# Gate-row indices, the row order of the modulation table, and the order of Pool's gathers and scatters in a mixture-of-experts stage

## The chip, the cores and the metric

The kernel runs on one core of a Trainium2 chip. The metric is the device time of one execution in microseconds (us). Before the change the median of three runs is 1618.47 us (1617.96 to 1618.78).

## The reference, cut to what matters

One decoder layer runs on 1024 prompt tokens and on 32 sample tokens (8 sequences of 4). A vector `c`, one for the prompt and one for each sample sequence, gives nine rows of modulation through `silu(c) @ w_ada + b_ada`: shift, scale and gate for the token mixers, and shift `sh2`, scale `sc2` and gate `g2` for the experts. After the mixers:

```python
h2 = rms_norm(x, norm2_g) * (1 + sc2) + sh2
y  = hier_moe(h2)                 # best group of 4, best 2 of its 8 experts, SwiGLU experts
x  = x + g2 * y                   # g2: one row for the prompt, one for each sample sequence
y_out = rms_norm(x, final_norm_g)
```

There are 32 experts with weights `w1`, `w3` (1024 x 512) and `w2` (512 x 1024) in float32, 6 MB for each expert. The 1056 tokens make 2112 assignments, 66 for an expert on average. With the inputs of this reference the lists are 24 to 172 tokens long.

## The kernel before, in words

The mixers run first, in two halves. The last stage, about 960 to 1616 us in the profile, is the expert stage: `moe_sync` (SyncE's queue, loads of weights), `moe_gpsimd` (Pool: indirect gathers and scatters), `moe_tensor`, `moe_scalar` and `moe_vector`. Each engine has its own list of instructions, in the order in which the code calls them, and waits on semaphores.

The stage goes through NB = 33 blocks of 128 slots. Blocks 0 to 31 are one for each expert, with its tokens in the first partitions, in the order of the tokens, and padding behind them (a padded slot holds token number 2047). Block 32 takes the rest of a list longer than 128. For a block `b`:

- Pool gathers the 128 token rows from `h2_rows` into `xg` (line 796, `gather`). Padded slots are out of bounds and are skipped.
- TensorE transposes them (line 904), ScalarE and VectorE split the result into a high part `xTh` and a low part `xTl`.
- Four chunks of `w1`/`w3` and two of `w2`, 1 MB each, come over SyncE's queue into a ring of 13 buffers `wr` (line 664). ScalarE rounds each to `whr` (`high`, line 1103), VectorE forms the rest `wl` (`low`, the helper at line 1288). TensorE multiplies three times for each product (lines 913 to 915 for the up part, 930 to 932 for the down part). A load waits until TensorE has freed its buffer.
- ScalarE multiplies the row of `g2` of each slot, held in `g2p`, by the slot's routing weight, into `gfac` (`factors`, line 1091). In block b's turn it does so for block b-1, ahead of two to four `high`. VectorE multiplies the product by `gfac` into `ysb` (`result`).
- Pool adds `ysb` to the residual rows `x_rows` in DRAM (line 800, `scatter`, an accumulating scatter).

`g2p` is one buffer. It is filled once with the prompt's row of g2 (line 849), and from then on it is patched: before each block an indirect gather (`gate_gather`, line 815) reads, by the index column `g2i[:, b]`, only the partitions whose row must change. Index 27 and above is out of bounds (`bounds_check=26`) and leaves the partition as it is. The source `gate_rows` is `mod_dram`, nine rows of three sections of 1024 (sh2, sc2, g2), seen as 27 rows: row 3n + 2 is the g2 of source n.

`gate_index` (line 1385) works out the indices. For 32 blocks at once it runs at the end of VectorE's block 0, just ahead of the `gate()` product of block 0 that TensorE waits for; for block 32 it runs once more in block 28. A slot with a sample token gets that sample's row; any other slot gets row 2 (the prompt) where the block before had a sample token in that partition, and else 30, which is skipped. So padding behaves as a prompt token does.

Pool's order is written out by hand. After the first three token gathers, for each block b: the token gather of b+3; for b = 0 the gate gather of block 0; the gate gather of b+1, once ScalarE has done factors(b); two table writes in blocks 3 to 11 (line 791); the scatter of b, once VectorE has done result(b). Behind the scatter of block 30 there stand a small weight gather (line 811), two gathers of residual rows (line 830) that wait for that scatter to land, and the gate gather of block 32. SyncE's loads of the residual tiles `yt` wait for the same scatter. The final norm and the stores follow.

Of the kernel before, what the change touches and what calls it, by code (L numbers as in the profile page):

```python
# [15 lines left out]
F32 = mybir.dt.float32  # L16
F32R = mybir.dt.float32r
BF16 = mybir.dt.bfloat16
I32 = mybir.dt.int32
U32 = mybir.dt.uint32  # L20
ALU = mybir.AluOpType
# [59 lines left out]
def build(nc, x_prompt, x_sample, c_prompt, c_sample, state_conv_a, state_conv_c, norm1_g, norm2_g,  # L81
# [5 lines left out]
    with ctx:  # L87
# [235 lines left out]
        eps, o = at("eps", [P, 1], F32, o)  # L323
# [47 lines left out]
        fss = sb("fss", [P, F_N])  # L371
        fv = sb("fv", [P, F_N])
        fr = sb("fr", [P, F_N])
        fy = sb("fy", [P, F_N])
        ft = sb("ft", [P, F_N])
# [402 lines left out]
        def moe_gpsimd(pool):  # L778
# [70 lines left out]
            pool.dma_start(g2p[:], mod_dram[0:1, 2 * D:3 * D].to_broadcast([P, D])).then_inc(g2_in, 16)  # L849
            for b in range(NB):  # L850
                if b + 3 < NB:
                    gather(b + 3)
                if b == 0:
                    pool.wait_ge(*gate_ok)
                    pool.wait_ge(g2_in, 16)
                    gate_gather(0, g2_in)
                if b + 1 < NB:
                    pool.wait_ge(m_w, b + 1)
                    gate_gather(b + 1, g2_in)
                if b == 3:  # L860
                    pool.wait_ge(dst_ok, 1)
                    pool.wait_ge(tab_out, 16)
                if 3 <= b < NT + 3:
                    fill_table(b - 3)
                if b < NB - 2:
                    scatter(b)
                if b == NT:
                    pool.wait_ge(wk_ok, 3)
                    pool.dma_start(wtab.rearrange("(p t) w -> p (t w)", p=P),
                                   wps[:].rearrange("p k t -> p (k t)")).then_inc(bd_in, 16)  # L870
                if b == NE - 2:
                    pool.wait_ge(bd_in, WT_IN + 16)
                    weight_gather(bd_in)
                if b == NB - 3:
                    base_gather(NB - 2)
                    base_gather(NB - 1)
# [409 lines left out]
        def moe_vector(dve):  # L1286
# [19 lines left out]
            dve.memset(wsl[:], 0.0)  # L1306
            pick_groups(dve, PT, NT)
# [77 lines left out]
            def gate_index(out, tok, before, now, n):  # L1385
                r, o = rf[:, 0:n], bf[:, 0:n]
                dve.tensor_scalar(r.bitcast(I32), tok, float(SEQ - TS), 0.0, ALU.subtract, ALU.max)
                dve.tensor_scalar(now, tok, float(SEQ), None, ALU.is_ge)
                dve.drain()
                dve.tensor_scalar(r.bitcast(I32), r.bitcast(I32), 2, None, ALU.logical_shift_right)  # L1390
                dve.scalar_tensor_tensor(now, tok, float(TOK), now, ALU.is_lt, ALU.mult)
                dve.drain()
                dve.tensor_scalar(r, r.bitcast(I32), 3.0, 2.0, ALU.mult, ALU.add)
                if before is None:
                    dve.memset(o, 2.0)
                else:
                    dve.tensor_scalar(o, before, 2.0 - 30.0, 30.0, ALU.mult, ALU.add)
                dve.drain()
                tt(r, r, o, ALU.subtract)
                dve.drain()  # L1400
                tt(r, r, now, ALU.mult)
                dve.drain()
                return tt(out, r, o, ALU.add)
# [66 lines left out]
            for b in range(NB):  # L1470
# [34 lines left out]
                if b == 0:  # L1505
                    table_rows_of()
                    dve.memset(gsf[:, 0:1], 0.0)
# [13 lines left out]
                if b == NB - 2:  # L1521
                    dve.memset(eps[:], EPS)
# [42 lines left out]
            with dve.If(n > 0):  # L1565
                scattered(dve, NB - 1)
                with dve.Fori(0, n) as i:
# [3 lines left out]
                    gate_index(g2i[:, NE:NB], xtok[:], None, gsf[:, NB:NB + 1], 1)  # L1571
# [86 lines left out]
        def _(pool):  # L1658
# [69 lines left out]
            def mod_store(i):  # L1728
# [3 lines left out]
                pool.dma_start(mod_dram[:, (j - 6) * 512:(j - 5) * 512], modr[:, i % 2, :]).then_inc(mod_out[i % 2], 16)  # L1732
# [60 lines left out]
            for g in range(2):  # L1793
# [26 lines left out]
                pool.dma_start(B2[:], mod_dram[0:1, 0:D].to_broadcast([P, D])).then_inc(ab_in, 16)  # L1820
                pool.dma_start(A2[:], mod_dram[0:1, D:2 * D].to_broadcast([P, D])).then_inc(ab_in, 16)
                if g:
                    pool.wait_ge(alo_ok, 2 * CW)
                    pool.wait_ge(st_out, 16 * (3 + 2 * NS))
                    for k in range(2):
                        for n in range(NS):
                            pool.dma_start(xs_s[n * TS:(n + 1) * TS, :] if k else xA[SMP + n * TS:SMP + (n + 1) * TS, PT, :],
                                           mod_dram[1 + n:2 + n, k * D:(k + 1) * D].to_broadcast([TS, D])
# [1453 lines left out]
```

## Time and profile before

| | us |
|---|---|
| median of 3 runs | 1618.47 |
| the profiled execution's own time | 1616.88 |
| its span | 1615.1 |
| TensorE busy | 1559.6 |
| VectorE busy | 1259.0 |
| ScalarE busy | 803.2 |
| Pool busy | 365.0 |

A page of the profile gives each engine's busy time, the span in 40 slices, and the chain of work that ended last. A timeline row is: start, duration, engine, line, operation, output<-input, count, and in brackets the idle time of the engine before it with the releaser. A row of the windows view gives the length of the stretch, then for TensorE, its weight loads, VectorE, ScalarE and Pool the busy time with the number of instructions, then the granted clock of TensorE as a share of full speed, the mean busy share of the 16 DMA engines, and GB/s. A DMA row ends with the median time from issue to landing, and a transfer has landed when the last of its parts has.

### The profile page before, as it was taken

Reading aid. Unit: us, or ns where it says so; the run is one execution under the profiler, and the core shown is the slowest. Engines: PE = TensorE matmul, PEld = TensorE weight load, DVE = VectorE, ACT = ScalarE, POOL = GpSimd, SP = SyncE. Lnnn points to the kernel's source line nnn. Section 1 sums busy time; section 2 is a strip of 40 time slices with the busy share of each in tenths; the row PEclk is TensorE's granted clock in tenths of the full one; section 3 lists DMA queues with packets and bytes.
Section 4 is the critical chain, followed back from the end, with each engine's and each line's share of the span. In section 5 each row is a group of like instructions: output and inputs, shape, how many; then the busy total and the mean of one; then the engine's idle time right before and its main releaser. Section 6 shows DMA issues by size and latency. Waiting matters only on the chain.

```text
span 1615.1 us, 23296 instructions
## 1 busy us (share of the span) xinstructions
PE 1559.6 (97%) x9097; PEld 1336.2 (83%) x9097; DVE 1259.0 (78%) x1703; ACT 803.2 (50%) x874; POOL 365.0 (23%) x273
## 2 busy tenths in 40 slices
PE   5999999999999999999999998999999999999993
PEld 3777788878889999999999977888888888888771
DVE  4668887755838898887555569999999999999985
ACT  4222232334333223313243356888788788777773
POOL 2310000000000000002000202466655544543231
PEclk9999999999999999999999998999999999999997
DMA  9965223424434332234222657999999999999965
GB/s 341 318 200 181 80 86 90 139 79 148 129 91 144 118 88 77 78 88 139 78 79 87 214 198 295 374 382 387 386 369 376 381 382 377 383 384 370 370 223 230
DMA packets 219025, 361.01 MB, mean 224 GB/s; under 512 B 20166, under 2 KB 168742, under 8 KB 193562
## 3 DMA queue, kind: packets, MB, share of 16 engines
q1 hardware_dynamic: 196476, 323.10, 55.8%
q0 software_dynamic: 21792, 34.25, 7.4%
q10 hardware_dynamic: 646, 2.15, 0.3%
q8 instruction: 73, 1.20, 0.3%
q14 instruction: 38, 0.31, 0.1%
HBM read 363.16 MB, written 32.34 MB: 245 GB/s over the span
## 4 chain that ended last, share of the span: by engine, by line
PE 85%; DMA 6%; DVE 5%; issue 1%; DVEq 1%; ACT 1%; POOL 0%; POOLq 0%; SPq 0%; ACTq 0%
PE z L2934 16%; PE z L2936 16%; PE z L2935 16%; PE z L913 6%; PE z L915 6%; PE z L914 6%; DMA wr<-in_w_dram 3%; PE z L930 3%; PE z L932 3%; PE z L931 3%; PE q L2825 2%; PE q L904 2%; PE q L2844 1%; DVE conv L2354 1%; DMA ada_h<-in_w_ada_dram 1%
## 5 line engine op out<-in xcount | busy, mean ns | idle before, releaser
L1288 DVE TENSOR_TENSOR wl<-wr,whr 128x2048 fp32r<-128x2048 f32 x196 | 442.2, 2284 | 0.1
L1103 ACT ACTIVATE whr<-wr 128x2048 fp32r<-128x2048 f32 x196 | 372.3, 1912 | 75.0 <-DMA wr<-in_w_dram 37.8
L2934 PE MATMUL z<-h_hi,w_hi 128*128 128x272 f32 (+1 forms) x1248 | 406.7, 326 | 2.3 <-DVE h_lo L2173 1.8
L2936 PE MATMUL z<-h_hi,w_lo 128*128 128x272 f32 (+1 forms) x1248 | 402.5, 322 | 0.0
L2935 PE MATMUL z<-h_lo,w_hi 128*128 128x272 f32 (+1 forms) x1248 | 401.3, 322 | 0.0
L2173 DVE TENSOR_TENSOR w_lo<-w_raw,w_hi 128x1024 fp32r<-128x1024 f32 (+1 forms) x168 | 179.4, 1068 | 127.4 <-ACT w_hi L1872 127.4
L2934 PEld LDWEIGHTS z<-h_hi,w_hi 128*128 128x128 f32 x1248 | 234.7, 188 | 28.3 <-issue 7.4
L2936 PEld LDWEIGHTS z<-h_hi,w_lo 128*128 128x128 f32 x1248 | 234.4, 188 | 16.6
L2935 PEld LDWEIGHTS z<-h_lo,w_hi 128*128 128x128 f32 x1248 | 234.8, 188 | 15.6 <-issue 0.2
L913 PE MATMUL z<-whr,xTh 128*128 128x512 f32 x528 | 209.9, 397 | 0.4 <-DVE xTl L1288 0.4
L915 PE MATMUL z<-wl,xTh 128*128 128x512 f32 x528 | 207.1, 392 | 0.0
L914 PE MATMUL z<-whr,xTl 128*128 128x512 f32 x528 | 206.5, 391 | 0.0
L2354 DVE SCALAR_TENSOR_TENSOR conv<-a_in,parT,conv 128x512 f32<-128x512 f32 x360 | 193.8, 582 | 14.5 <-issue 1.3
L1872 ACT ACTIVATE w_hi<-w_raw 128x1024 fp32r<-128x1024 f32 (+1 forms) x168 | 150.3, 929 | 48.1 <-DMA w_raw<-in_w_in_dram 48.0
L2050 ACT ACTIVATE sig<-z 128x512 f32<-128x512 f32 (+1 forms) x48 | 29.3, 611 | 264.9 <-PE z L2936 264.9
L815 POOL DMA_INDIRECT g2p<-mod_rows,g2i x33 | 82.8, 2509 | 250.6 <-ACT gfac L1091 232.9
L915 PEld LDWEIGHTS z<-wl,xTh 128*128 128x128 f32 x528 | 99.7, 189 | 21.4
L913 PEld LDWEIGHTS z<-whr,xTh 128*128 128x128 f32 x528 | 100.1, 190 | 20.2 <-DVE xTl L1288 0.6
L914 PEld LDWEIGHTS z<-whr,xTl 128*128 128x128 f32 x528 | 99.8, 189 | 19.8
L930 PE MATMUL z<-whr,gTh 128*128 128x512 f32 x256 | 102.7, 401 | 3.2 <-DVE gTl L1288 3.2
L932 PE MATMUL z<-wl,gTh 128*128 128x512 f32 x256 | 100.0, 391 | 0.0
L931 PE MATMUL z<-whr,gTl 128*128 128x512 f32 x256 | 99.9, 390 | 0.0
(483 smaller groups left out, 2304.6 us busy)
## 6 DMA issues: line engine op xcount, KB each, us to landing
wr<-in_w_dram SPq DMA_DIRECT2D x198, 1024.0 KB, 17.4
w_raw<-in_w_in_dram SPq DMA_DIRECT2D x104, 512.0 KB, 3.8
ada<-in_w_ada_dram SPq DMA_DIRECT2D x6, 2048.0 KB, 14.4
w_raw<-in_w_branch_dram SPq DMA_DIRECT2D x48, 256.0 KB, 2.8
w_raw<-in_w_out_dram SPq DMA_DIRECT2D x16, 512.0 KB, 4.0
ada_h<-in_w_ada_dram SPq DMA_DIRECT2D x2, 2048.0 KB, 15.1
ada_u<-in_w_ada_dram SPq DMA_DIRECT2D x2, 2048.0 KB, 9.9
ada_m<-in_w_ada_dram SPq DMA_DIRECT2D x2, 2048.0 KB, 10.8
```

The source lines that it names most:

```text
L913: pe.matmul(out, xTh[s][:, k, :], hi[:, i * FF:(i + 1) * FF], start=(k == 0), stop=False)
L914: pe.matmul(out, xTl[s][:, k, :], hi[:, i * FF:(i + 1) * FF], start=False, stop=False)
L915: last = pe.matmul(out, xTh[s][:, k, :], lo[:, i * FF:(i + 1) * FF], start=False, stop=(k == KD - 1))
L930: pe.matmul(out, gTh[:, k, :], hi[:, w0:w0 + 512], start=(k == 0), stop=False)
L1103: act.activation(whr[n % HN][:], wr[n % RN][:], ACT.Copy).then_inc(m_hi, 1)
L1288: return dve.tensor_tensor(out, a, b, op)
L1872: act.activation(w_hi[n % WS][:, 0:kn, :], w_raw[n % WS][:, 0:kn, :], ACT.Copy).then_inc(whi_ok, 1)
L2173: return dve.tensor_tensor(out, a, b, op)
L2354: last = dve.scalar_tensor_tensor(out, x, wt, out, ALU.mult, ALU.add)
L2934: pe.matmul(out, w_hi[w][:, k, :], hi[:, k, t0:t1], start=(k == 0), stop=False)
L2935: pe.matmul(out, w_hi[w][:, k, :], lo[:, k, t0:t1], start=False, stop=False)
L2936: last = pe.matmul(out, w_lo[w][:, k, :], hi[:, k, t0:t1], start=False, stop=(k == kn - 1))
```

## The change

`mod_dram` is stored with its three sections in another order: g2, sh2, sc2. Row 3n is now the g2 of source n, and all readers of the sections are moved accordingly. `gate_index` shrinks from nine operations in six steps, each closed by a drain, to five in three. The index is now 3 x source for a sample token; for a prompt token 0 where the block before did not have a prompt token in that partition, and 30 (skipped) where it had; padding comes out at 27 or more and is skipped. Pool does the gate gather of block 0 ahead of the token gather of block 3, and in each block the scatter of b ahead of the gate gather of b+1. A memset of `eps` moves from block 31 to the head of the stage, and one memset of a zero column joins it.

```diff
             pool.wait_ge(xg0_ok, 2)
             gather(1)
             gather(2)
-            pool.dma_start(g2p[:], mod_dram[0:1, 2 * D:3 * D].to_broadcast([P, D])).then_inc(g2_in, 16)
+            pool.dma_start(g2p[:], mod_dram[0:1, 0:D].to_broadcast([P, D])).then_inc(g2_in, 16)
+            pool.wait_ge(*gate_ok)
+            pool.wait_ge(g2_in, 16)
+            gate_gather(0, g2_in)
             for b in range(NB):
                 if b + 3 < NB:
                     gather(b + 3)
-                if b == 0:
-                    pool.wait_ge(*gate_ok)
-                    pool.wait_ge(g2_in, 16)
-                    gate_gather(0, g2_in)
-                if b + 1 < NB:
-                    pool.wait_ge(m_w, b + 1)
-                    gate_gather(b + 1, g2_in)
                 if b == 3:
                     pool.wait_ge(dst_ok, 1)
                     pool.wait_ge(tab_out, 16)
...
                 if b < NB - 2:
                     scatter(b)
+                if b + 1 < NB:
+                    pool.wait_ge(m_w, b + 1)
+                    gate_gather(b + 1, g2_in)
...
+            dve.memset(none[:], 0.0)
+            dve.memset(eps[:], EPS)
...
             def gate_index(out, tok, before, now, n):
                 r, o = rf[:, 0:n], bf[:, 0:n]
                 dve.tensor_scalar(r.bitcast(I32), tok, float(SEQ - TS), 0.0, ALU.subtract, ALU.max)
-                dve.tensor_scalar(now, tok, float(SEQ), None, ALU.is_ge)
+                dve.tensor_scalar(now, tok, float(SEQ), None, ALU.is_lt)
                 dve.drain()
                 dve.tensor_scalar(r.bitcast(I32), r.bitcast(I32), 2, None, ALU.logical_shift_right)
-                dve.scalar_tensor_tensor(now, tok, float(TOK), now, ALU.is_lt, ALU.mult)
+                dve.scalar_tensor_tensor(o, before, 30.0, now, ALU.mult, ALU.mult)
                 dve.drain()
-                dve.tensor_scalar(r, r.bitcast(I32), 3.0, 2.0, ALU.mult, ALU.add)
-                if before is None:
-                    dve.memset(o, 2.0)
-                else:
-                    dve.tensor_scalar(o, before, 2.0 - 30.0, 30.0, ALU.mult, ALU.add)
-                dve.drain()
-                tt(r, r, o, ALU.subtract)
-                dve.drain()
-                tt(r, r, now, ALU.mult)
-                dve.drain()
-                return tt(out, r, o, ALU.add)
+                return dve.scalar_tensor_tensor(out, r.bitcast(I32), 3.0, o, ALU.mult, ALU.add)
...
-                    dve.memset(gsf[:, 0:1], 0.0)
+                    dve.memset(gsf[:, 0:1], 1.0)
...
                 if b == NB - 2:
-                    dve.memset(eps[:], EPS)
                     dve.wait_ge(*row_pr)
...
-                pool.dma_start(mod_dram[:, (j - 6) * 512:(j - 5) * 512], modr[:, i % 2, :]).then_inc(mod_out[i % 2], 16)
+                pool.dma_start(mod_dram[:, (j - 10) % 6 * 512:(j - 10) % 6 * 512 + 512], modr[:, i % 2, :]).then_inc(mod_out[i % 2], 16)
...
-                pool.dma_start(B2[:], mod_dram[0:1, 0:D].to_broadcast([P, D])).then_inc(ab_in, 16)
-                pool.dma_start(A2[:], mod_dram[0:1, D:2 * D].to_broadcast([P, D])).then_inc(ab_in, 16)
+                pool.dma_start(B2[:], mod_dram[0:1, D:2 * D].to_broadcast([P, D])).then_inc(ab_in, 16)
+                pool.dma_start(A2[:], mod_dram[0:1, 2 * D:3 * D].to_broadcast([P, D])).then_inc(ab_in, 16)
```

## Rows read from the trace of the kernel before

**Rows 1.** The page: the chain that ended last, by engine.

```profile
PE 85%; DMA 6%; DVE 5%; issue 1%; DVEq 1%; ACT 1%; POOL 0%; POOLq 0%; SPq 0%; ACTq 0%
```

**Rows 2.** Windows view of three stretches: end of block 0, start of block 1, steady blocks.

```profile
1001.00:1003.80 2.80, 0.00 (x0) 0.00 (x0) 2.31 (x14) 0.00 (x0) 0.00 (x0) 0.87 1.01 423
1003.80:1010.00 6.20, 6.16 (x18) 4.92 (x19) 6.20 (x4) 2.40 (x2) 2.90 (x1) 0.51 1.01 425
...
1200.00:1300.00 100.00, 100.00 (x477) 83.90 (x476) 95.50 (x58) 80.94 (x58) 51.02 (x20) 1.00 0.99 378
```

**Rows 3.** DMA view, weight loads of 1010 to 1050, 1230 to 1400, 1450 to 1540.

```profile
wr<-in_w_dram SPq DMA_DIRECT2D x14, 1024.0 KB, 7.8
...
wr<-in_w_dram SPq DMA_DIRECT2D x58, 1024.0 KB, 20.0
...
wr<-in_w_dram SPq DMA_DIRECT2D x29, 1024.0 KB, 25.6
```

**Rows 4.** Waits of 1450 to 1540: us in total, times, longest.

```profile
ACT whr L1103 <- DMA wr<-in_w_dram: 21.1, 30, 1.5
```

**Rows 5.** VectorE's timeline at the end of block 0.

```profile
1001.38 0.18 DVE L1387 TENSOR_SCALAR rf<-tok 128x32 int32<-128x32 int32 x1
...
1002.07 0.18 DVE L1393 TENSOR_SCALAR rf<-rf 128x32 f32<-128x32 int32 x1
...
1002.95 0.19 DVE L1288 TENSOR_TENSOR g2i<-rf,bf 128x32 int32<-128x32 f32 x1
1003.06 0.68 DVE L1288 TENSOR_TENSOR gs<-hsg,z 128x512 f32<-128x512 f32 x1
```

**Rows 6.** Pool's timeline: gate gather of block 1, then one steady block.

```profile
1015.60 2.91 POOL L815 DMA_INDIRECT g2p<-mod_rows,g2i  x1 [8.79 <-ACT gfac L1091]
...
1229.02 2.91 POOL L815 DMA_INDIRECT g2p<-mod_rows,g2i  x1 [5.47 <-ACT gfac L1091]
1232.98 2.89 POOL L800 DMA_INDIRECT x_rows<-ysb,tok  x1 [1.06 <-DVE ysb L1288]
1236.18 2.91 POOL L796 DMA_INDIRECT xg<-h_rows,tok  x1 [0.30 <-issue]
1246.75 2.92 POOL L815 DMA_INDIRECT g2p<-mod_rows,g2i  x1 [7.66 <-ACT gfac L1091]
```

**Rows 7.** ScalarE's timeline in the same block.

```profile
1228.13 3.71 ACT L1103 ACTIVATE whr<-wr 128x2048 fp32r<-128x2048 f32 x2
...
1244.84 1.14 ACT L1091 ACTIVATE gfac<-g2p,wslot 128x1024 f32<-128x1024 f32 x1
```

**Rows 8.** VectorE's timeline in the same block.

```profile
1230.96 1.22 DVE L1288 TENSOR_TENSOR ysb<-z,gfac 128x1024 f32<-128x1024 f32 x1
1232.10 2.28 DVE L1288 TENSOR_TENSOR wl<-wr,whr 128x2048 fp32r<-128x2048 f32 x1
```

**Rows 9.** Source view, landing times of all scatters (line 800), then token gathers (796).

```profile
DMA to landing us min/median/max: 6.8/11.5/12.7
...
DMA to landing us min/median/max: 5.4/12.0/12.2
```

**Rows 10.** The chain that ended last, two pieces of its last part: start, duration.

```profile
1559.66 6.77 DMA x_rows<-ysb,tok
...
1571.08 10.97 DMA g2p<-mod_rows,g2i
```

**Rows 11.** Pool's timeline near the end.

```profile
1555.95 2.04 POOL L815 DMA_INDIRECT g2p<-mod_rows,g2i  x1 [12.94 <-ACT gfac L1091]
1559.66 2.22 POOL L800 DMA_INDIRECT x_rows<-ysb,tok  x1 [1.67 <-issue]
```

**Rows 12.** VectorE's timeline near the end.

```profile
1557.00 1.22 DVE L1288 TENSOR_TENSOR ysb<-z,gfac 128x1024 f32<-128x1024 f32 x1
...
1560.37 0.06 DVE L1522 MEMSET eps<- 128x1 f32 x1
```

**Rows 13.** ScalarE's timeline near the end.

```profile
1566.82 1.14 ACT L1091 ACTIVATE gfac<-g2p,wslot 128x1024 f32<-128x1024 f32 x1
```

More of the change, by code:

```diff
@@ L322, in build @@
         same, o = at("same", [P, P], F32, o)
-        eps, o = at("eps", [P, 1], F32, o)
         assert o <= slot_at[4]
@@ L370, in build @@
         tbn = sb("tbn", [P, NE])
[L371 to L375, printed above, removed]
+        fin = sb("fin", [P, 5 * F_N + 4])
+        fss = fin[:, 0:F_N + 1]
+        fv, fr, fy, ft = (fin[:, i * F_N + 1:(i + 1) * F_N + 1] for i in range(1, 5))
+        eps, none, ehalf = (fin[:, 5 * F_N + i:5 * F_N + i + 1] for i in range(1, 4))
         wslot = sb("wslot", [P, NE])
@@ L1570, in moe_vector @@
                     dve.drain()
-                    gate_index(g2i[:, NE:NB], xtok[:], None, gsf[:, NB:NB + 1], 1)
+                    gate_index(g2i[:, NE:NB], xtok[:], none[:], gsf[:, NB:NB + 1], 1)
                     weight_rows(xw[:, 0:1], xw[:, 1:2], xcol[:]).then_inc(o_c, 1)
@@ L1827, in _ @@
                             pool.dma_start(xs_s[n * TS:(n + 1) * TS, :] if k else xA[SMP + n * TS:SMP + (n + 1) * TS, PT, :],
-                                           mod_dram[1 + n:2 + n, k * D:(k + 1) * D].to_broadcast([TS, D])
+                                           mod_dram[1 + n:2 + n, (k + 1) * D:(k + 2) * D].to_broadcast([TS, D])
                                            ).then_inc(abs_in, 16)
```

## The prediction, made before the changed kernel was run

> **What bounds the kernel now.** I read the page first: 85% of the chain that ended last is TensorE's own [rows 1]. A change that touches only indices and Pool's order can then pay in three places: where TensorE stands still, where the weights come too late, and in the tail behind the last products.
>
> The windows view shows the one large hole of the expert stage. From 1001.0 to 1003.8 us TensorE runs nothing, and in the 6.2 us after it, 18 matmuls take 6.16 us at a granted clock of 0.51, the lower level of 1.2 GHz [rows 2]. VectorE's timeline says why: TensorE waits for gs, and gs starts at 1003.06, right behind the last operation of the gate indices at 1002.95 [rows 5]. This index chain is on the path.
>
> In the steady blocks TensorE has no gap (100.00 of 100 us) while VectorE is busy 95.5 [rows 2]; a block takes 17.73 us, from gate gather to gate gather [rows 6]. But the loads fall behind. The median time to landing of a 1 MB chunk goes from 7.8 to 20.0 to 25.6 us [rows 3], with the DMA engines busy 0.99 of the time [rows 2], and from about 1450 us ScalarE waits for a chunk 30 times, 21.1 us in 90 [rows 4]. So TensorE sets the pace at first, uses up the lead of the 13 buffers, and at the end the DMA engines set it. A transfer lands when its last part does, so it is the fullest of the 16 engines that counts. This decides how each edit is priced: whatever TensorE gains early moves everything behind it, but work added to the fullest DMA engine anywhere in the stage moves the end too.
>
> The tail hangs on Pool: the chain goes through the scatter of block 30 (1559.66, 6.77 us to land), the two residual gathers, and the gate gather of block 32 (1571.08, 10.97 us) [rows 10].
>
> **The change part by part.**
>
> *Fewer index operations, block 0.* The kept operations of the first two steps stay where they are. The new last operation stands where the third step starts now, at 1002.07, instead of 1002.95 [rows 5]. That is 0.88 us less, and gs, TensorE and all behind them start 0.88 earlier. The same code runs in block 28 for one column; it saves about as much on VectorE there, but this is the part in which the weights come late [rows 4], so I count 0. Were that cover gone it would be another 0.9 gained. gs also waits for TensorE's product, which ended by 1001.0 [rows 2], so nothing else is next in line. Term: -0.9.
>
> *The two memsets at the head.* One as it now stands takes 0.06 us [rows 12]. Two more on the head of VectorE's routing chain cost 0.04 to 0.12; the one gone from block 31 is not waited for. Term: +0.1.
>
> *Rows that are fetched again.* This isn't visible in the list of operations. Before, padding counted as "prompt row still there". Now a prompt token behind a padded slot reads row 0 again, though g2p holds it. I counted both rules on the routing that the reference gives for its inputs: 122 rows of 4 KB before, 481 after, 359 more over 33 blocks (105 in block 4, where a list of 172 follows one of 24; 70 in block 19). At 378 GB/s, or 23.6 for each of 16 engines [rows 2], one row takes 4096 / 23.6 = 0.17 us of one engine. Which engine serves which partition no row shows. Bounds: 0 if they all fall on engines with room, and 359 / 16 x 0.17 = 3.9 us if spread evenly; were the fullest engine to carry the largest share that a grouping in neighbouring partitions gives, about 50 rows, it would be 8.5. I take 2.0, below the even share. The lists fill the low partitions in every block (the shortest has 24), so the fullest engines serve low partitions, and a low partition was never padding before. The new rows lie above the end of the preceding list. Term: +2.0 (0 to 3.9).
>
> The Trainium skill, "DMA: Bandwidth & Descriptors", section "The descriptor swizzle", gives the partitions of each engine in a 128-partition transfer: engine 0 has 0 to 3 and 32 to 35, and so on in fours. By it engine 0 is the fullest (502 real rows in gathers and scatters before) and gets 14 more, 2.4 us. No view here shows the engines one by one, so I keep it beside the sum, which would be 0.4 higher.
>
> *Scatter ahead of the gate gather, steady blocks.* In the present order a scatter starts 0.80 us after its result ends (1232.18, then 1232.98) [rows 6, 8], so it gains nothing by going first. The gate gather goes from 1229.02 to the place of the token gather, 1236.18, and that one to about 1239.4 [rows 6]. Behind the gate gather ScalarE's gfac waits, next due at 1244.84, and behind gfac on ScalarE two rounds of weights [rows 7]. The rows of the gate gather now queue behind the scatter's. A scatter needs 11.5 us to land (to 1244.5), and the token gather that stands in that place now needs 12.0 (to 1248.2) [rows 9]. Between these, and nearer to the first because most of its slots are skipped: 1246, so gfac waits about 1.1 us (0 to 3.4). What covers it: the first weight round behind gfac ends half-way through the pair at 1228.13 + 1.86 = 1229.99, and VectorE takes it at 1232.10 [rows 7, 8], 2.1 us later. Result waits for gfac too, with 1230.96 - (1244.84 + 1.14 - 17.73) = 2.7. So 1.1 disappears, and stable: the next scatter depends on result, which isn't late. The token gather, 3.2 us later, lands by about 1252, and its transpose comes in the turn after the next. In the table blocks (3 to 11) the two table writes move behind scatter and gate gather; nobody waits for them. Term: 0.
>
> *Gate gather of block 0 first.* It waits for the indices, now 0.9 earlier; the token gather of block 3 behind it is needed two blocks later. Term: 0.
>
> *Tail.* Result(30) ends at 1558.22 [rows 12], and the scatter starts at 1559.66, 1.44 later, since Pool has just finished a gate gather [rows 11]. With the usual 0.80 it starts 0.64 earlier, with no gather's slots ahead of it in the queue; for that I add 0.3 (0 to 1). The gate gather of block 31 goes behind it, at about 1561.5, and its gfac is due at 1566.82 [rows 13]; the scatter issued ahead of it needs 6.77 to land [rows 10], to about 1565.8, so it lands at about 1567 and may hold gfac by 1 us. The gate gather of block 32 needs that gfac, but stands behind the residual gathers until about 1570 and doesn't wait. Term: -0.9 (-1.6 to +0.5).
>
> Sum: -0.9 + 0.1 + 2.0 + 0 - 0.9 = +0.3, on the profiled execution 1616.88 to 1617.2. Its own time is 1.59 below the median of the runs; on the median, 1618.47 + 0.3 = 1618.8.
>
> **The rivals.**
>
> *The clock stays up.* With the index chain 0.88 shorter TensorE stands still for 2.0 instead of 2.85 us. The clock fell at this hole; if it doesn't after a shorter one, the 6.2 us at 0.51 would take 3.2, up to 3.0 less. VectorE then holds TensorE (two weight rounds of 2.28 each stand behind gs before the low part that the down product needs), so I take 2.0. Time: 1616.8, and 1614.8 where the fetched rows cost nothing as well. For it: the hole is a third shorter. Against it: it is still the longest in the stage.
>
> *The fetched rows are hidden.* The sum is then -1.7: 1616.8.
>
> *The queue of the gate gather holds ScalarE.* This is the one that ends slower: the gate rows land as late as a token gather does now, or later. It decides from a wait of 2.1 us in gfac, plus the 0.8 that VectorE has free in a block (4.5% of 17.73 [rows 2]). At the bound of 3.4 us 0.5 is left, and blocks of 18.2 instead of 17.73: over 30 blocks 547 against the 540.4 that they take now (1015.60 to 1555.95, gate gathers of blocks 1 and 31 [rows 6, 11]), +7, less the 1.7 of the other terms: 1623.8. Against it: most slots of this gather move nothing.
>
> The Trainium skill, same page, section "Queues, rings and completion order", has one ring for each queue and engine, worked through in order, and turns taken between queues. By that the gate rows cannot pass the scatter's, which speaks for this rival; the present rows fit it, but a landing time for the gate gathers they don't give.
>
> *The rows fall on the fullest engine.* 8.5 instead of 2.0: 1625.3.
>
> *The change doesn't shorten the path*, since something else holds gs: +0.9, 1619.7, inside the forecast's range.
>
> **How the numbers follow.** Forecast (with the last rival) 0.52, its own range 1616.4 to 1621.2; clock up 0.22, of which a half goes below 1615.2; rows hidden 0.08; queue 0.09; fullest engine 0.09. A measurement of this kernel can tell about 0.2%, 3.2 us, from no change: faster is under 1615.2, slower over 1621.7. Faster: 0.11 + 0.03 + 0.03 from sums of small gains = 0.17. Slower: 0.18 + 0.01 = 0.19. Same: 0.64. The range leaves out a tenth on each side: 1614.6 to 1623.6.
>
> **What would show it.** In the changed profile: the hole before line 921 at 1001 is 2.0 us long; the granted clock behind it is either near 0.5 or 1.0, which settles the first rival. In steady blocks the period is still 17.7, gfac waits about 1 us for the DMA of g2p, and the second weight round of VectorE shows no new wait on ScalarE. ScalarE's waits for weights begin a little earlier than 1450 and the median landing of the last blocks is a little above 25.6, if the rows cost; unchanged, if they are hidden. In the tail the scatter of block 30 starts 0.8 behind its result. The prediction is wrong if the steady period changes, if gfac waits more than 2.9 us, or if the last weights land more than 4 us later or earlier than the sum lets them.

## The result, and the profile after

| | before | after |
|---|---|---|
| median | 1617.18 (20 runs, 1616.28 to 1620.70) | 1620.86 (20 runs, 1618.53 to 1623.40) |
| ratio, with its 95% interval | | 1.0020 (1.0014 to 1.0026) |
| the profiled execution's own time | 1616.88 | 1621.35 |
| its span | 1615.1 | 1619.6 |

The changed kernel is slower by 3.2 us by the ratio and 3.7 by the medians. That lies inside the range (1614.6 to 1623.6) and on the bound of 0.2% between "same" and "slower". The forecast of 1618.8 was 2 us too low, and part of that nearness is luck: it stood on a median of three runs, 1.3 us above that of twenty (moved down by 1.3, the range still holds the result). The change itself was forecast at +0.3 and measured at +3.7 (3.2 by the ratio). The sum of small terms behind it hides one that was badly wrong.

**The gate rows hold ScalarE in every block.** The waits of 1018 to 1450 us, changed kernel (total us, times, longest):

```profile
ACT gfac L1088 <- DMA g2p<-mod_rows,g2i: 93.0, 23, 4.8
...
DVE wl L1285 <- ACT whr L1100: 11.3, 22, 0.5
```

Before, gfac waited once, 5.4 us in all; now about 4 us in every block but 31 (129.8 us in 32 over the stage). VectorE pays 0.5 of it in nearly every block, behind the first weight round: the new wait that the prediction had asked to look for. The timelines of Pool, ScalarE and VectorE in a steady block, changed kernel:

```profile
1238.52 3.51 POOL L798 DMA_INDIRECT x_rows<-ysb,tok  x1 [10.03 <-DVE ysb L1285]
1242.33 1.92 POOL L813 DMA_INDIRECT g2p<-mod_rows,g2i  x1 [0.30 <-issue]
1244.55 1.85 POOL L794 DMA_INDIRECT xg<-h_rows,tok  x1 [0.30 <-issue]
...
1252.89 1.16 ACT L1088 ACTIVATE gfac<-g2p,wslot 128x1024 f32<-128x1024 f32 x1 [3.75 <-DMA g2p<-mod_rows,g2i]
...
1254.14 1.23 DVE L1285 TENSOR_TENSOR ysb<-z,gfac 128x1024 f32<-128x1024 f32 x1 [0.27 <-issue]
1255.89 2.29 DVE L1285 TENSOR_TENSOR wl<-wr,whr 128x2048 fp32r<-128x2048 f32 x1 [0.53 <-ACT whr L1100]
...
1256.16 3.50 POOL L798 DMA_INDIRECT x_rows<-ysb,tok  x1 [9.76 <-DVE ysb L1285]
```

These rows make a ring. The scatter starts at 1238.52, the gate gather 3.81 behind it, gfac when that has landed (10.56 later), result 1.25 behind gfac, and the next scatter 2.02 behind result: 17.64 us in this block; from gfac to gfac the blocks take 17.0 to 19.4, mean 18.2 (544.81 / 30), as the landing time varies. Nothing of TensorE is in it. Compare [rows 6], where the gate gather starts 3.96 ahead of the scatter (1229.02, 1232.98) and not 3.81 behind it.

**The loads are no longer waited for.** DMA view, weight loads of 1010 to 1050, 1230 to 1400 and 1450 to 1540, then the windows row of the steady stretch, all of the changed kernel; they answer to [rows 2, 3]:

```profile
wr<-in_w_dram SPq DMA_DIRECT2D x13, 1024.0 KB, 9.4
...
wr<-in_w_dram SPq DMA_DIRECT2D x57, 1024.0 KB, 14.4
...
wr<-in_w_dram SPq DMA_DIRECT2D x29, 1024.0 KB, 20.5
...
1200.00:1300.00 100.00, 99.98 (x474) 83.49 (x473) 93.78 (x57) 80.18 (x59) 49.10 (x20) 1.00 1.00 375
```

ScalarE's waits for a chunk between 1450 and 1540 [rows 4] are gone. So the blocks become slower early and faster late. VectorE's timelines, the starts of result in blocks 0, 21 and 30, first before, then after:

```profile
1017.57 1.22 DVE L1288 TENSOR_TENSOR ysb<-z,gfac 128x1024 f32<-128x1024 f32 x1
...
1390.74 1.22 DVE L1288 TENSOR_TENSOR ysb<-z,gfac 128x1024 f32<-128x1024 f32 x1
...
1557.00 1.22 DVE L1288 TENSOR_TENSOR ysb<-z,gfac 128x1024 f32<-128x1024 f32 x1
```

```profile
1016.86 1.22 DVE L1285 TENSOR_TENSOR ysb<-z,gfac 128x1024 f32<-128x1024 f32 x1
...
1397.92 1.23 DVE L1285 TENSOR_TENSOR ysb<-z,gfac 128x1024 f32<-128x1024 f32 x1 [0.61 <-issue]
...
1561.00 1.22 DVE L1285 TENSOR_TENSOR ysb<-z,gfac 128x1024 f32<-128x1024 f32 x1 [0.62 <-issue]
```

The distance is -0.7, then +7.2, then +4.0 us. A block of the first 21 takes 18.15 (381.06 / 21) in place of 17.77; one of the next nine 18.12 (163.08 / 9) in place of 18.47. The ring costs 7.9 us, and 3.2 come back, since the old kernel lost time here to late weights and the new one doesn't. The starts of gfac (1386.87 and 1396.68 in block 21, 9.8 apart) would mislead: gfac stood 3.9 us ahead of result before and stands 1.2 ahead now, so part of its delay is slack used up, and no time.

**Block 0.** Windows of the changed kernel around the hole ahead of the gate product, and one earlier; then TensorE's row at the hole and VectorE's at the indices:

```profile
1001.00:1004.30 3.30, 1.31 (x7) 0.78 (x5) 2.90 (x13) 0.61 (x1) 0.00 (x0) 1.00 1.01 425
1004.30:1010.00 5.70, 5.12 (x27) 4.32 (x28) 5.70 (x4) 4.29 (x5) 4.79 (x2) 1.00 1.02 428
982.80:986.20 3.40, 3.02 (x24) 2.97 (x24) 1.12 (x2) 1.02 (x1) 0.30 (x1) 0.50 0.82 269
...
1004.30 0.72 PE L918 MATMUL q<-ident,gs 128*128 128x128 f32 x4 [1.99 <-issue]
...
1002.71 0.18 DVE L1386 TENSOR_SCALAR rf<-tok 128x32 int32<-128x32 int32 x1
...
1003.40 0.19 DVE L1392 SCALAR_TENSOR_TENSOR g2i<-rf,bf 128x32 int32<-128x32 int32 x1
1003.51 0.68 DVE L1285 TENSOR_TENSOR gs<-hsg,z 128x512 f32<-128x512 f32 x1
```

From the first index operation to gs it is 0.80 us where [rows 5] have 1.68: the 0.88 of the sum. The hole is 1.99 long and the granted clock stays at 1.00 behind it, but from 982.8 to 986.2 it is 0.50, where before it was 1.00, and the first index operation starts 1.33 later (1001.38, 1002.71). So the gate product of block 0 starts 0.46 later than before (1003.84, 1004.30), but that of block 1 starts 1.40 earlier (1024.42, 1023.02): 1.86 us are gained in the block behind the hole, where the clock now stays up.

**The tail.** The chain that ended last, changed kernel, its pieces that answer to [rows 10], and Pool's row behind the scatter:

```profile
1548.84 10.84 DMA g2p<-mod_rows,g2i
...
1563.09 7.81 DMA x_rows<-ysb,tok
...
1575.70 10.85 DMA g2p<-mod_rows,g2i
...
1566.81 1.02 POOL L813 DMA_INDIRECT g2p<-mod_rows,g2i  x1 [0.30 <-issue]
```

The gate gathers stand on the chain now. The tail isn't shorter. Result(30) is 4.0 us later than before and the end of the span 4.5. The scatter starts 2.09 behind the start of its result, where before it was 2.66 (1557.00, 1559.66), but it lands in 7.81 in place of 6.77 [rows 10]: 0.57 gained, 1.04 lost.

### The profile page after: what moved, and what is told of

Read it like the earlier page. It is cut to its first block, busy times and chain, and to the rows that moved or that the text cites. A ratio compares the mean times of both kernels' runs of the same rounds, so it can differ in the third digit from the quotient of the medians.

```text
span 1619.6 us, 23283 instructions
## 1 busy us (share of the span) xinstructions
PE 1560.7 (96%) x9097; PEld 1334.9 (82%) x9097; DVE 1256.9 (78%) x1696; ACT 790.4 (49%) x874; POOL 368.0 (23%) x273
## 4 chain that ended last, share of the span: by engine, by line
PE 77%; DVE 8%; DMA 7%; issue 3%; ACT 1%; SPq 1%; DVEq 1%; POOL 1%; POOLq 0%; ACTq 0%
PE z L2922 16%; PE z L2924 16%; PE z L2923 16%; DMA g2p<-mod_rows,g2i 5%; PE z L912 4%; PE z L910 4%; PE z L911 4%; DVE wl L1285 3%; PE z L927 3%; PE z L929 3%; PE z L928 3%; PE q L2813 2%; DVE conv L2342 1%; PE q L901 1%; DMA w_raw<-in_w_in_dram 1%
## 5 line engine op out<-in xcount | busy, mean ns | idle before, releaser
L1100 ACT ACTIVATE whr<-wr 128x2048 fp32r<-128x2048 f32 x196 | 363.6, 1903 | 5.1 <-PE z L912 5.1
L2922 PEld LDWEIGHTS z<-h_hi,w_hi 128*128 128x128 f32 x1248 | 234.7, 188 | 28.8 <-issue 8.0
L798 POOL DMA_INDIRECT x_rows<-ysb,tok x31 | 106.5, 3434 | 260.4 <-DVE ysb L1285 249.5
```

Source lines behind the costliest of these rows:

```text
L1100: act.activation(whr[n % HN][:], wr[n % RN][:], ACT.Copy).then_inc(m_hi, 1)
L2922: pe.matmul(out, w_hi[w][:, k, :], hi[:, k, t0:t1], start=(k == 0), stop=False)
```

## The experiments

In five of the profiled executions below (the order alone, the gate gather first, the indices moved, and the first and third of the last three kernels) TensorE's clock falls once more in the very last block, to 0.50, and the span is longer for it, by some 1.9 us with the indices moved (from result(30) to the end 60.0, where before it was 58.1). Times are therefore compared by the medians.

**The two halves of the change.** First only Pool's order:

```diff
+            pool.wait_ge(*gate_ok)
+            pool.wait_ge(g2_in, 16)
+            gate_gather(0, g2_in)
             for b in range(NB):
...
-                if b + 1 < NB:
-                    pool.wait_ge(m_w, b + 1)
-                    gate_gather(b + 1, g2_in)
...
                 if b < NB - 2:
                     scatter(b)
+                if b + 1 < NB:
+                    pool.wait_ge(m_w, b + 1)
+                    gate_gather(b + 1, g2_in)
```

> The kernel before with only Pool's order of the change (scatter of b ahead of the gate gather of b+1, first gate gather ahead of the fourth token gather); indices and rows read as before. Theory 1, a closed loop: the gate gather now starts only after the result of its block and lands behind the scatter's rows, gfac waits for it, result waits for gfac, and the scatter for result; the changed kernel's own trace has 3.8 us from scatter to gate gather, 10.8 to its landing and 3.2 for gfac, result and the start of the next scatter, 17.8 to 18 per block. Then this kernel alone shows the whole loss and, without the 0.9 us that shorter indices save, 4 to 6 us over before, with gfac waiting about 4 us in each block. Theory 2, the refetched rows are the loss: this kernel is at before within 1 us, and gfac waits under 1.5 us.

Measured: 1620.3 beside 1617.73 before, ratio 1.0015 (1.0006 to 1.0024). Row of gfac's releaser in the source view:

```profile
  DMA g2p<-mod_rows,g2i: 116.9, 32
```

Then only the indices and their rows of the table: the changed kernel with those Pool lines put back.

> The changed kernel with Pool's order of before: five-operation indices, 481 rows read instead of 122. Theory 1: no wait of gfac in the steady blocks, period 17.75 us; the index chain saves 0.9 us, up to 3 more if the clock stays up behind the shorter hole, and the rows cost 0 to 2.4 as the prediction had it; -3 to +1.5 against before. Theory 2: +3 to +5, weights landing later than 25.6 us in the last blocks.

Measured: 1620.28, ratio 1.0015 (1.0006 to 1.0023). gfac waits 8.2 us in two. Weight loads of 1450 to 1540 and ScalarE's wait for them in that stretch:

```profile
wr<-in_w_dram SPq DMA_DIRECT2D x29, 1024.0 KB, 26.0
...
ACT whr L1101 <- DMA wr<-in_w_dram: 20.5, 29, 1.5
```

In this stretch it looks like before. But ScalarE now waits for chunks early: 19.8 us between 1310 and 1400, where before it was 1.5 between 1018 and 1380. TensorE, 1.70 ahead of before in block 16 (gate products at 1289.36 and 1291.06), is 2.90 behind in block 30 (1546.32, 1543.42).

Each half alone costs about 2.6 us, both together 3.2 to 3.7 and not 5.2. The order makes gfac wait and the weights early; the indices make the weights late. They use the same slack from two ends. With the order alone the first 21 blocks lose 6.8 us (result from 1017.42 to 1397.41), in the changed kernel 7.9, so some 1.1 of that goes with the fetched rows or with chance between two executions.

**The price of a fetched row.** In the kernel with the indices alone, all prompt slots fetch again, 2112 rows in place of 481:

```diff
-                dve.scalar_tensor_tensor(o, before, 30.0, now, ALU.mult, ALU.mult)
+                dve.scalar_tensor_tensor(o, before, 0.0, now, ALU.mult, ALU.mult)
```

> As the kernel with the indices alone, but every prompt slot reads row 0 again in each block: 2112 rows instead of 481. It prices a row. If rows were spread evenly over the 16 engines: 1631 / 16 x 0.17 = 17 us over the kernel with the indices alone. If it is the fullest engine that counts and the skill's partition table holds (Trainium skill, DMA: Bandwidth & Descriptors, The descriptor swizzle), that engine gets 234 more rows, 40 us. If it is none of them that set the end: within 2 us.

Measured: 1658.21, 37.9 above the kernel with the indices alone; the loads of 1450 to 1540 land in 28.8. 1631 rows more, spread evenly over 16 engines, would be 102 each and 17 us at the 0.17 us of a row that the prediction worked out. It is more than twice that. Either the uneven share counts, or a row costs over twice the 0.17; this run alone can't say which. Dealing out the same rows, further below, speaks for the share.

The Trainium skill, "DMA: Bandwidth & Descriptors", "The descriptor swizzle", gives the partitions of each engine. By that grouping, an estimate, the fullest engine gets 234 of the 1631 rows, and 37.9 / 234 = 0.162 us for each. The measured time agrees with the page, since this is close to 0.17; no view shows the engines one by one.

**Behind the scatter, or only later?** In the kernel with the indices alone the gate gather also waits for the result, but stays ahead of the scatter in the queue:

```diff
                 if b + 1 < NB:
                     pool.wait_ge(m_w, b + 1)
+                    if b < NB - 2:
+                        pool.wait_ge(m_y, b + 1)
                     gate_gather(b + 1, g2_in)
```

> The kernel with the indices alone, but the gate gather of b+1 also waits for the result of block b, and goes ahead of the scatter: as late as in the changed kernel to within 3.8 us, but with no scatter ahead of it in the queue. Theory 1a, it is the scatter's rows ahead of it: it lands 9.2 us after its issue as before, 12 us after the result, and gfac waits 0 to 1 us; time within 1.5 us of the indices alone. Theory 1b, it is being issued behind the result at all: gfac waits 3 us or more and the time is at the changed kernel's.

Measured: 1622.77 (1620.03 to 1626.47), ratio 1.0032 (1.0021 to 1.0044). ScalarE's wait at gfac over the whole kernel:

```profile
ACT gfac L1091 <- DMA g2p<-mod_rows,g2i: 9.0, 2, 6.3
```

Landing time of the gate gathers there (least, median, most):

```profile
DMA to landing us min/median/max: 5.3/8.6/11.3
```

Issued about 4 us later than with the indices alone, the gather is still never waited for, apart from the two waits that were there. What makes gfac late is the place behind the scatter, and it takes both of its parts: the 3.8 us until Pool is done with the scatter, and the rows ahead in the queue, with which the gather lands in 10.9 and not 8.6. Here it starts 11.8 ahead of gfac; 3.8 later it would have 8.0 left, and with 8.6 to land gfac would wait 0.6, an estimate, which the slack covers.

This kernel is 2.5 us slower than the one with the indices alone, and the intervals just overlap. In the profiled executions (spans 1621.0 and 1618.5) the two are level as far as the gate product of block 32, at 1584.31 and 1584.32. All of the difference lies behind it, where the clock falls to 0.50 in this one and not in the other. Whether that is so in the other runs, no record tells.

**A longer ring.** The changed kernel with eight memsets and a drain on Pool between scatter and gate gather:

```diff
+        spare = sb("spare", [P, 8])
...
                     scatter(b)
                 if b + 1 < NB:
+                    for i in range(8):
+                        pool.memset(spare[:, i:i + 1], 0.0)
+                    pool.drain()
                     pool.wait_ge(m_w, b + 1)
                     gate_gather(b + 1, g2_in)
```

> The changed kernel with eight small memsets and a drain on Pool between each scatter and the gate gather behind it, some 0.7 to 1.2 us in all, work of no use. Theory 1, the closed loop scatter, gate gather, gfac, result, scatter sets the block's pace: every block gets longer by the whole delay, 31 blocks, +20 to +35 us over the changed kernel, and gfac's wait grows by as much. Rival, the gate gather has room and the loss is in the DMA engines: gfac's wait grows, the period doesn't, within 2 us of the changed kernel.

Measured: 1711.44, ratio 1.0589 (1.0567 to 1.0610). Pool's timeline, one block:

```profile
1234.59 1.58 POOL L799 DMA_INDIRECT x_rows<-ysb,tok  x1 [0.30 <-issue]
1235.60 0.89 POOL L864 MEMSET spare<- 128x1 f32 x8
1246.02 2.71 POOL L814 DMA_INDIRECT g2p<-mod_rows,g2i  x1 [9.53 <-issue]
```

The delay was far longer than meant: in this block the gate gather starts 11.4 us behind the scatter, not 3.8, and what the drain stood for, no row shows. So this run can't give the price of a microsecond on the ring; of some 7 us of delay in a block 2.9 show in the time (90.6 / 31), in blocks that mostly alternate between about 17.5 and 25 us (16.2 to 27.4). In most of the short ones gfac starts 4 to 6 us behind the issue of its gate gather and not 10.9, so a part of the delay is paid back by a quick landing; why only every other block gets that was not followed up. The sign is clear: a delay between the two reaches the end.

**Block 0 alone.** The kernel before, with the index operations moved out of TensorE's way, ahead of the expert stage's loop:

```diff
+            dve.memset(gsf[:, 0:1], 0.0)
+            dve.drain()
+            gate_index(g2i[:, 0:NE], tok0[:], gsf[:, 0:NE], gsf[:, 1:NE + 1], NE).then_inc(gate_ok[0], 1)
             dve.wait_ge(m_xT, 1)
...
-                    dve.memset(gsf[:, 0:1], 0.0)
-                    dve.drain()
-                    gate_index(g2i[:, 0:NE], tok0[:], gsf[:, 0:NE], gsf[:, 1:NE + 1], NE).then_inc(gate_ok[0], 1)
```

> The kernel before, rows and Pool's order untouched, with its nine index operations moved ahead of the loop into the time in which VectorE waits for the first high part (1.4 us idle there); the hole of TensorE at the end of block 0 shrinks from 2.85 to about 1 us. If TensorE's path sets the end: 1.5 to 4 us faster than before. If the fullest DMA engine sets it, what TensorE gains in block 0 only makes the weights queue longer: the loads of 1010 to 1050 land later than 7.8 us and the time is -1.5 to 0.

Measured: 1617.47 beside 1617.12, ratio 1.0001 (0.9992 to 1.0010). The hole goes:

```profile
1002.76 0.72 PE L921 MATMUL q<-ident,gs 128*128 128x128 f32 x4 [0.60 <-issue]
```

It is 0.60 long in place of 2.85, the clock behind it stays at 1.00, and the time doesn't move. (The counts of two semaphores are changed to match; the cut leaves them out.) Where the gain goes, TensorE's timelines show: the gate products of blocks 16 and 30, first before, then here.

```profile
1291.06 0.63 PE L921 MATMUL q<-ident,gs 128*128 128x128 f32 x4
...
1543.42 0.63 PE L921 MATMUL q<-ident,gs 128*128 128x128 f32 x4
```

```profile
1288.12 0.63 PE L921 MATMUL q<-ident,gs 128*128 128x128 f32 x4
...
1542.91 0.63 PE L921 MATMUL q<-ident,gs 128*128 128x128 f32 x4
```

TensorE is 2.94 us ahead from block 1 to block 16, and 0.51 in block 30: the lead is given back where the weights come late.

**The tail alone.** In block 30 only, the scatter ahead of the gate gather, first in the kernel with the indices alone, then in the one with the indices moved:

```diff
-                if b + 1 < NB:
+                if b + 1 < NB and b != NB - 3:
...
+                if b == NB - 3:
+                    pool.wait_ge(m_w, b + 1)
+                    gate_gather(b + 1, g2_in)
```

> The kernel with the indices alone, and in block 30 only the scatter ahead of the gate gather. The prediction's tail term: -0.6 to -1.6 against the indices alone. If the gate gather of block 31, now behind the scatter, holds gfac and with it the gate gather of block 32: 0 or slower.

> The kernel before with both: indices moved ahead of the loop, and in block 30 the scatter ahead of the gate gather. The sum of the two: -0.6 to -3 against before; the candidate for a version that beats both kernels.

Measured: 1619.24 (1.0 below the kernel it was made from) and 1617.26 (0.2 below). Both are inside the spread of the runs, so the times decide nothing about the 0.9 of the sum. The traces do. The scatter of block 30 on the chain, start and time to land: indices alone, then with the tail's order; indices moved, then with the tail's order.

```profile
1562.88 6.67 DMA x_rows<-ysb,tok
...
1560.96 7.30 DMA x_rows<-ysb,tok
```

```profile
1559.32 6.65 DMA x_rows<-ysb,tok
...
1558.74 7.49 DMA x_rows<-ysb,tok
```

Behind the start of result it begins 2.08 in both, in place of 2.67 and 2.66, and lands 0.63 and 0.84 more slowly. From result to landing nothing is gained: 9.38 for 9.34, and 9.57 for 9.31.

**Slots dealt out over the DMA engines.** If the fullest engine sets the end, the cure is to level it. One pattern changes which partition a slot number has; the same rows move:

```diff
-            pool.iota(io128[:], pattern=[[1, P]], base=0, channel_multiplier=0,
+            pool.iota(io128[:], pattern=[[8, 2], [64, 2], [1, 8], [16, 4]], base=0, channel_multiplier=0,
```

In the kernel before:

> The kernel before with the slots of a block dealt out over the partitions in another order (one iota's pattern), so that a short list no longer lies in the low partitions. Everything else, also the number of rows moved, is as before. Theory A (the fullest of the 16 DMA engines sets the end, so work added to it costs in full): the blocks of the last third keep the 17.7 to 17.8 us of the first ones in place of 18.6 to 18.8, ScalarE's waits for chunks after 1450 (21.1 us in 30) go to under 5, the median landing of a chunk stays under 12 us to the end, and the time is 6 to 9 us below before: 0.994 to 0.996. Theory B (all engines together are the bound, or TensorE): 0.999 to 1.001 and the median landing of the last chunks stays at 24 to 26. By the Trainium skill, DMA: Bandwidth & Descriptors, The descriptor swizzle, the fullest engine has 302 real rows of gathers and scatters then in place of 502; at the 0.162 us a row that the study with all prompt rows fetched gave, that would be 32 us of one engine, more than enough for theory A.

In the changed kernel:

> The changed kernel with the same dealing out of the slots. Theory A (in the changed kernel the loop scatter, gate gather, gfac, result sets the block, about 18 us, and the DMA engines no longer bound it): the loop becomes shorter only as far as scatter and gate gather land earlier on less uneven engines. The gate gather lands 10.8 us behind its issue now; if 1 us of it goes, the gfac waits fall from 4 to about 3 us a block and the time by up to 10 us, to 1610 to 1616; if it lands as late as now, the time stays within 3 us of the changed kernel's 1620.9 and is then 8 to 12 us above the kernel before with the same dealing out. Theory B (the loop is no bound, the loss was fetched rows on the fullest engine): as fast as the kernel before with the slots dealt out, within 1 us.

And in the kernel with moved indices and the tail's order:

> The kernel before with three edits: the index operations ahead of the gate's wait, the scatter of block 30 ahead of the gate gather of block 31, and the slots dealt out. The first two alone came out at 1617.26 (ratio 1.0002). Theory A: those two gained nothing because the fullest DMA engine set the end; with the slots dealt out TensorE's path does, so they now count: 1.5 to 4 us below the kernel before with only the slots dealt out (0.9 to 2.2 of the hole before G(0), with what the clock gives back, and 0.6 to 1.5 in the tail). Theory B: they are worth nothing on any path: within 1 us of it.

| | median (5 runs, before 9) | ratio to before |
|---|---|---|
| before | 1616.83 | |
| before, dealt out | 1609.85 | 0.9955 (0.9942 to 0.9969) |
| changed, dealt out | 1608.20 | 0.9946 (0.9932 to 0.9959) |
| indices moved, tail, dealt out | 1607.77 | 0.9942 (0.9929 to 0.9956) |

In the first of them the weights are on time to the end. The loads of 1230 to 1400 and of 1450 to 1540, and the windows row of the late stretch:

```profile
wr<-in_w_dram SPq DMA_DIRECT2D x58, 1024.0 KB, 7.0
...
wr<-in_w_dram SPq DMA_DIRECT2D x29, 1024.0 KB, 7.6
...
1450.00:1540.00 90.00, 89.98 (x428) 75.31 (x427) 86.46 (x66) 72.28 (x52) 37.65 (x15) 1.00 1.00 383
```

ScalarE has no wait for a chunk left after 1450, TensorE has no gap, and 7 us are gone, as theory A had it. The rows and bytes are the same; only their partitions differ. That the limit is the fullest DMA engine, and not something else that goes by partition, is inferred: no view shows the engines one by one. In the changed kernel so dealt, gfac waits less, and the gate gather's landing shows why. Waits of 1018 to 1450, then the gate gathers' landing times (least, median, most), first the changed kernel's own, then with the slots dealt out:

```profile
ACT gfac L1088 <- DMA g2p<-mod_rows,g2i: 57.6, 24, 5.0
```

```profile
DMA to landing us min/median/max: 4.3/10.9/12.2
```

```profile
DMA to landing us min/median/max: 4.2/10.0/13.0
```

Its time is then 1.6 us below that of the kernel before with the same dealing, with intervals that overlap. In the profiled executions TensorE's gate product is 1.26 ahead of that kernel in block 5 (1093.16, 1094.42), 1.46 behind in block 8 (1149.14, 1147.68) and 1.17 behind in block 30. So the ring still costs 2.7 us in three blocks, where gfac waits up to 5.0; at a mean wait of 2.4 us it isn't the bound elsewhere. The expectation that it would still lose 8 to 12 if it landed as late was not put to the test, since it landed 0.9 earlier.

The third is 2.1 below the first (1.5 to 4 expected), 1606.83 to 1609.01 against 1608.50 to 1611.32; with five runs each that isn't certain, but the traces say the same. TensorE's gate product is 1.79 ahead of the first in block 1 (1021.27, 1023.06) and still 1.79 ahead in block 30 (1536.97, 1538.76), where in the kernel with the moved indices alone the lead was lost. The scatter of block 30 starts 0.57 sooner behind its result and lands as before (7.07, 7.06). What TensorE gains early counts once the weights are on time. It is the fastest kernel here, though not distinct from the changed one with the slots dealt out.

**The clock once more.** The kernel before, unchanged:

> The kernel before, unchanged, profiled again for the granted clock in block 0. If the two stretches at about 0.5 lie at one place for one program (after the hole ahead of G(0) and at 972 to 979), the clock answers to what the program does there. If they move by several us between two executions of the same program, then the kernel with the shorter hole that kept its clock there does not show that a shorter hole keeps it.

Measured: one run of 1618.28. The clock falls at the same two places, up to 979.5 and behind the same hole. Windows row behind the hole:

```profile
1003.80:1010.00 6.20, 5.80 (x16) 4.78 (x17) 6.20 (x5) 2.40 (x2) 2.90 (x1) 0.50 1.01 424
```

But the kernel with only Pool's order, which has the same index chain, had a hole of 2.04 and its clock at 1.00 as it ended, then at 0.64 from 1006 to 1010; and the dealt-out kernel before, with a hole of 1.94, went to 0.50 from 1004.5 to 1006. A hole of 2 us is thus seen with the clock falling behind it and without. Nearly all the kernels whose clock stays up here lose it for some 3 us between 979.5 and 990 instead, or before 976. What decides stays open.

## Why the prediction was right, and where it wasn't

- *What bounds the kernel.* Right, and shown: "work added to the fullest DMA engine anywhere in the stage moves the end too" (refetching, +37.9; dealing out, -7), with the fullest engine inferred. Half of the sentence was wrong: "whatever TensorE gains early moves everything behind it". While late weights set the end, TensorE's gains are worth nothing (2.2 us of hole gone, 2.94 of lead in block 16, 0.51 in block 30, ratio 1.0001). The late weights also begin sooner than "from about 1450": ScalarE had waited 11.8 us for them between 1380 and 1450.
- *Block 0, -0.9.* The 0.88 is there in the rows. It isn't in the time, for the reason just given. The error is the pricing, not the duration. "The clock stays up" happened at this hole, and its price of 2.0 was good: the block behind it gained 1.86. The chain of indices had started 1.33 later, with the clock down from 982.8 to 986.2, and the path wasn't TensorE's, so the end shows nothing of it.
- *Memsets, +0.1.* Too small to be seen.
- *Fetched rows, +2.0.* The indices alone measured about +2.6 with the 0.9 worth nothing, so the size was right to about half a microsecond, and the rival of 8.5 is out. By the grouping that the Trainium skill's page gives, an estimate, 14 of the 359 new rows fall on the fullest engine where an even share is 22, and at 0.162 they cost 2.3. That bears out the reason given for a value below the even share (new rows lie high, the fullest engines serve low partitions).
- *Scatter ahead of the gate gather, 0.* This is the step that failed. gfac waits 4.1 us (129.8 / 32), not 1.1, and above the bound of 3.4. Two terms were mis-sized. The gate gather starts 1242.33 - 1238.52 = 3.8 behind the scatter, since Pool is busy 3.5 with it now, where [rows 6] gave 3.2; and it lands 10.9 later (median), against 9.0 with the indices alone. I had put it "nearer to the first because most of its slots are skipped"; behind the scatter it took nearly the token gather's 12.0. And "stable: the next scatter depends on result, which isn't late" overlooked that result depends on gfac, gfac on the gather and the gather on the scatter: from 2.9 us of wait on, that ring is the period. By the prediction's own signs (a changed steady period, a wait above 2.9) this makes it wrong, although the time lies inside its range.
- *The rival "the queue of the gate gather holds ScalarE"* had the mechanism and the threshold (2.1 + 0.8) right. Dealt out, the wait is 2.4 and nearly free; as changed it is 4.1 and the early blocks take 18.15. Its price of 7 was net, for thirty blocks set against what they take with the late weights. From result(0) to result(30) they took 544.14 in place of 539.43: +4.7, of blocks of 18.14 and not 18.2. With 0.09 it was rated too low.
- *Tail, -0.9.* Wrong, by its second part. The scatter started 0.86 behind the end of its result (1562.23, 1563.09), as said, and 0.57 sooner than before. But "with no gather's slots ahead of it" it was to land 0.3 faster, and it landed 0.6 to 1.0 more slowly in all three pairs of kernels without dealt-out slots. From result(30) to the end the changed kernel is 0.5 longer.

In the profiled executions the whole is -0.7 at result(0), +7.9 to block 21, -3.2 to block 30 and +0.5 in the tail, together the +4.5 of the spans. So the forecast was near for partly wrong reasons: an omitted loss of 7.9 in the ring, of which 3.2 came back, savings in block 0 and the tail that weren't paid, and a base that was 1.3 too high.

## What to carry to other kernels

Before an indirect transfer is moved behind another on its queue, follow its consumer until the circle closes: if the consumer feeds what must be issued first, the landing time of the one and the issue time of the other add up to a period, and the test is that period against the block, not the wait against the idle time. Where the loads fall behind, look at how the real rows lie in the partitions: with short lists all in the low ones, permuting the slots was worth 7 us here, more than anything the change touched. Two edits that each lose time against the same slack don't add up, and neither do gains on an engine that doesn't set the end. And measure a delay on what the path runs through: gfac's start was later by 9.8 us where result's was later by 7.2.

## What the runs showed of the hardware that I had not expected

- The median landing of 1 MB chunks was 25.6 us between 1450 and 1540 and 7.6 with the same bytes dealt out, with the DMA engines' mean busy share at 1.00 both times. The mean share doesn't tell whether one of them is behind.
- The scatter takes Pool 3.5 us as changed, where it follows 10 us of idle time, and 2.9 in the order of before [rows 6], with the same rows. The idle time alone doesn't explain it: in the changed kernel with the slots dealt out it is 2.9 (median) behind 8 us of idle time. Why, no run tells.
- A skipped slot still makes a packet. The page's packet lines of before and after differ by one packet in all, while 358 fewer are under 512 bytes and 1.47 MB more are moved, the 359 rows of 4 KB. And in the kernel before with the slots dealt out the gate gathers need 9.0 us to land (median) with 122 real rows in 33 gathers, and the token gathers 10.5 with 2112.

```profile
DMA packets 219025, 361.01 MB, mean 224 GB/s; under 512 B 20166, under 2 KB 168742, under 8 KB 193562
```

```profile
DMA packets 219026, 362.48 MB, mean 224 GB/s; under 512 B 19808, under 2 KB 168384, under 8 KB 193563
```

- Eight memsets and a drain behind a scatter kept Pool from its gate gather for 5.2 to 9.5 us in neighbouring blocks (idle time ahead of the gathers at 1267.76 and 1246.02).
